# Block 0 of a hybrid layer on one core: who computes the convolution taps, when the transposes run, who scales the norms, and the order of the first norm

## The reference

```
h  = rmsnorm(x, g_mix_pre)
z  = h @ w_in                                   # GLU value | gate | q | k | v | o | i | f
a  = z[GLU value] * sigmoid(z[GLU gate])
a  = causal depthwise conv, width 31 (a) + b    # 512 channels
a  = silu(group_layernorm(a, 4 groups of 128 channels))
hm = group_layernorm(mLSTM(q, k, v, i, f), per head) * sigmoid(o)   # 4 heads, chunkwise
x += rmsnorm(concat(a, hm) @ w_out)
```

## Time and profile before

| | us |
|---|---|
| median of 3 runs | 2807.46 |
| lowest, highest | 2803.95, 2808.06 |
| the profiled execution, its own time | 2811.34 |
| its span in the profile | 2809.4 |
| PE busy | 2710.0 (96%) |
| DVE busy | 1701.6 (61%) |
| ACT busy | 914.6 (33%) |
| POOL busy | 225.7 (8%), all in block 0 |

### The profile page before, as it was taken

The page is one execution under the profiler, slowest core; times in us unless marked ns, Lnnn a source line. Parts: engine busy times, 40 slices in busy tenths (PEclk is TensorE's granted clock), DMA queues, the critical chain, the costliest instruction groups (busy, mean ns, idle before and its releaser), DMA issues.

```text
span 2809.4 us, 37471 instructions
## 1 busy us (share of the span) xinstructions
PE 2710.0 (96%) x14657; PEld 2605.9 (93%) x14657; DVE 1701.6 (61%) x3648; ACT 914.6 (33%) x1851; POOL 225.7 (8%) x93
## 2 busy tenths in 40 slices
PE   6989999999999999999999999999999999899998
PEld 6879999988999999998999999999999998799998
DVE  6976677775646846536566655555766636472644
ACT  5344433444532112424321223443112325211113
POOL 4322433412000000000000000000000000000000
PEclk9999999999999999999999999999999999899999
DMA  8746889987456666574666666556666576366665
GB/s 283 284 158 244 314 324 337 327 301 265 179 214 232 232 230 234 200 278 163 227 231 231 234 225 220 227 201 225 229 236 224 213 279 143 128 249 227 237 226 194
DMA packets 109563, 660.57 MB, mean 235 GB/s; under 512 B 20283, under 2 KB 20927, under 8 KB 39631
## 3 DMA queue, kind: packets, MB, share of 16 engines
q1 hardware_dynamic: 100238, 628.84, 62.6%
q10 hardware_dynamic: 9152, 29.36, 2.8%
HBM read 533.04 MB, written 125.11 MB: 234 GB/s over the span
## 4 chain that ended last, share of the span: by engine, by line
PE 74%; DVE 8%; DMA 8%; ACT 4%; POOL 3%; issue 1%; POOLq 0%; SPq 0%; DVEq 0%; ACTq 0%
PE proj L635 23%; PE proj L636 22%; PE proj L637 22%; DMA w_raw<-in_w_units 7%; POOL w_split L619 3%; ACT w_split L990 1%; DVE mix_room L1578 1%; DMA w_split<-w_kept 1%; DVE cv L1700 1%; PE m L752 1%; DVE small L1797 1%; PE m L668 1%; PE m L792 1%; DVE w_split L2162 1%; PE m L798 1%
## 5 line engine op out<-in xcount | busy, mean ns | idle before, releaser
L635 PE MATMUL proj<-h_split,w_split 128*128 128x416 f32 x2720 | 977.6, 359 | 22.0 <-DVE h_split L1583 7.1
L636 PE MATMUL proj<-h_split,w_split 128*128 128x416 f32 x2720 | 953.9, 351 | 0.0
L637 PE MATMUL proj<-h_split,w_split 128*128 128x416 f32 x2720 | 948.6, 349 | 0.0
L635 PE MATMUL proj<-f_split,w_split 128*128 128x416 f32 x1568 | 565.1, 360 | 32.9 <-DVE f_split L1832 11.6
L636 PE MATMUL proj<-f_split,w_split 128*128 128x416 f32 x1568 | 552.5, 352 | 0.0
L637 PE MATMUL proj<-f_split,w_split 128*128 128x416 f32 x1568 | 549.2, 350 | 0.0
L635 PEld LDWEIGHTS proj<-h_split,w_split 128*128 128x128 f32 x2720 | 511.2, 188 | 37.6 <-issue 19.9
L637 PEld LDWEIGHTS proj<-h_split,w_split 128*128 128x128 f32 x2720 | 512.1, 188 | 9.8
L636 PEld LDWEIGHTS proj<-h_split,w_split 128*128 128x128 f32 x2720 | 512.7, 188 | 3.0 <-issue 0.8
L635 PEld LDWEIGHTS proj<-f_split,w_split 128*128 128x128 f32 x1568 | 296.2, 189 | 54.1 <-DVE f_split L1832 15.1
L1700 DVE SCALAR_TENSOR_TENSOR cv<-a_ext,vecs,cv 128x416 f32<-128x416 f32 (+1 forms) x510 | 315.2, 669 | 0.0
(11 more groups left out here) (270 smaller groups left out, 2184.8 us busy)
## 6 DMA issues: line engine op xcount, KB each, us to landing
w_split<-w_kept SPq DMA_DIRECT2D x432, 1024.0 KB, 4.8
w_kept<-w_split SPq DMA_DIRECT2D x108, 1024.0 KB, 7.8
w_raw<-in_w_units SPq DMA_DIRECT2D x108, 512.0 KB, 5.7
x_resid<-in_x ACTq DMA_DIRECT2D x5, 1664.0 KB, 12.5
out_y<-x_resid ACTq DMA_DIRECT2D x8, 832.0 KB, 9.0
rows<-in_x ACTq DMA_DIRECT2D x4, 832.0 KB, 8.1
w_raw<-in_x ACTq DMA_DIRECT2D x3, 832.0 KB, 11.5
qkv<-in_p ACTq DMA_DIRECT2D x5, 416.0 KB, 5.3
```

The lines of the kernel that those rows point to most:

```text
L635: mm(dst, w_hi, a_hi, start=first, stop=False)
L636: mm(dst, w_hi, a_lo, start=False, stop=False)
L637: return mm(dst, w_lo, a_hi, start=False, stop=last)
```

## The change

It has four parts, all in block 0.

1. *Convolution.* The first 15 taps of channel tile 3 go from PE to DVE; PE keeps 16, now 3, 4, 3, 3 and 3 in the five places instead of 6, 8, 5, 6 and 6. DVE adds PE's sum to its own. Until tap 21, 20 and 10 the partial sums of tiles 0, 1 and 2 lie in the PSUM banks m1, m3 and m4, which the heads need from step A of head 0 on; PE waits for that there (`s_taps`).
2. *Transposes.* T1 moves from group 20 to group 21, behind step A of head 2; within group 23, T2 moves later by two products. Its first transpose waits for all four convolution tiles.
3. *Norm scaling.* ACT scales half of batch 0 and all three tiles of batch 1 (`shifted`), which needs a shift computed by DVE.
4. *First norm.* DVE makes the low part of weight unit 0 in place of POOL; ACT makes the high part of unit 1 ahead of the high parts of h; scaling and low parts alternate; groups 0 and 1 are computed product by product in turn; a small square root at the start of ACT's list loads its table.

```diff
-TURNS_FIRST, TURNS, TURNS_LAST = {"T1": 20, "T2": 23}, {"T1": 17, "T2": 20}, {"T1": 17, "T2": 21}
+TURNS_FIRST, TURNS, TURNS_LAST = {"T1": 21, "T2": 23}, {"T1": 17, "T2": 20}, {"T1": 17, "T2": 21}
+PRODUCTS_FROM = 15
-PRODUCTS_CONV = (range(6), range(6, 14), range(14, 19), range(19, 25), range(25, CW))
+PRODUCTS_CONV = (range(15, 18), range(18, 22), range(22, 25), range(25, 28), range(28, CW))
+TAPS_BANK = [(c, k) for n in range(5) for c, k in ((0, 16 + n), (2, 2 * n), (1, 16 + n), (2, 2 * n + 1))] + [(0, 21), (2, 10)]
+BANK_END = {0: 21, 1: 20, 2: 10}
-TURN_ENDS = (22, 28, 36, 43, 49, 57, 61)
+TURN_ENDS = (8, 14, 24, 31, 37, 47, 54)
...
+            two_groups(0, False, 0, h, lambda n: pe.wait_ge(s_h.sem, s_h.done(0, n + 1)))
             for i in range(FRONT):
-                group(0, False, i, h, ...)
+                if i > 1:
+                    group(0, False, i, h)
...
                     pe.wait_ge(s_evac.sem, s_evac.done(blk, 12 + 3 * i + 3))
+                    if first and i == 0:
+                        pe.wait_ge(s_taps.sem, len(BANK_END))
...
+                    if split and i == 2:
+                        shifted(0, (2, 3))
+                    elif split and i == H - 1:
+                        shifted(1, (5, 6))
...
+                def tap_first(c, k, last_of):
+                    bank = {0: m1, 1: m3, 2: m4}.get(c)
+                    end = BANK_END.get(c, -1)
+                    home, kept = (bank[:, 0:T] if k < n else cv[:, c, :] for n in (end, end + 1))
...
+                        ins = v.scalar_tensor_tensor(home, a_ext[:, c, k:k + T], wt, kept, ALU.mult, ALU.add)
...
+                    if part == len(TURN_ENDS) - 1:
+                        dve.wait_ge(s_convp.sem, 1)
+                        v.tensor_tensor(cv[:, DIAGONAL, :], cv[:, DIAGONAL, :], m5[:, 0:T], ALU.add).then_inc(s_conv.sem, 1)
...
                     inverse_root(0)
+                    dve.wait_ge(s_hi.sem, 1)
+                    v.tensor_tensor(w[:, 0, 1, :], w_raw[:, 0, :], w[:, 0, 0, :].bitcast(F32),
+                                    ALU.subtract).then_inc(s_w[0].sem, 16)
                     dve.wait_ge(s_rb.sem, s_rb.done(blk, 1))
-                    normalise_next(0, range(KD))
+                    for i in range(KD + 4):
+                        if i < KD:
+                            v.scalar_tensor_tensor(x_next(i), x_next(i), col("g_mix_pre", i), m2[:, 0:T], ...)
+                        if i >= 4:
+                            low_next(0, [i - 4])
...
                     batch_stats(0)
+                    batch_factor(0)
+                    batch_apply(0, (0, 1))
                     head_c(2)
```

More of the change, by code:

```diff
@@ L620, in low_part @@
                                         ALU.subtract).then_inc(s_w[slot].sem, 16)
-            for r in range(SPLITS):
+            for r in range(1, SPLITS):
                 if r not in SPLIT_ON_VECTOR:
@@ L870, in program @@
                             for c in range(CT):
-                                then[min(2 * c + 2, KD - 1) if last else 2 * c] = lambda c=c: turn(c)
+                                late = last or first and i == turns["T2"]
+                                then[min(2 * c + 2, KD - 1) if late else 2 * c] = lambda c=c: turn(c)
                         if last and i in (17, 20, 23):
@@ L1060, in _ @@
             root(0, 0, m5, 1)
+            high_part(1)
             for i in range(KD):
                 high_h(0, 0, 0, i, h, x_next(i))
-            for u in range(1, RING):
+            for u in range(2, RING):
                 high_part(u)
@@ L1070, in _ @@
                 front_group(0, 0, i, True)
[L1071 removed]
+                diagonals(range(PRODUCTS_FROM + 2 * i, min(PRODUCTS_FROM + 2 * i + 2, CW)))
             gate_rows(0, 0)
@@ L1115, in shifted @@
                 def shifted(batch, tiles):
-                    act.wait_ge(s_lnshift.sem, batch + 1)
+                    act.wait_ge(s_lnshift.sem, (2 if last else 0) + batch + 1)
+                    if split and batch == 0:
+                        act.wait_ge(s_ln.sem, s_ln.done(blk, 2))
                     for k, (tile, n, size) in enumerate(pieces_of(batch, last)):
@@ L1122, in shifted @@
                         ins = fn(src, src, ACT.Identity, bias=ln_shift[0:size, k:k + 1], scale=ln_rs[0:size, k:k + 1])
-                        if n == (4 if batch else NCH - 1):
+                        if n == (4 if batch and last else NCH - 1):
                             ins.then_inc(s_ln.sem, 1)
@@ L1249, in program @@
                             next_squares(range(6, KD))
-                        elif last and i == 1:
+                        elif not mid and i == 1:
                             shifted(1, (4,))
@@ L1811, in batch_factor @@
                     link(v.reciprocal(ln_rs[0:LC, 0:n], ln_std[0:LC, 0:n]))
-                    if last and batch < 2:
+                    if not mid and batch < 2:
                         v.scalar_tensor_tensor(ln_shift[0:LC, 0:n], ln_mv[0:LC, 0:n, 0], -1.0, ln_rs[0:LC, 0:n], ALU.mult,
@@ new lines, in program @@
+                    head_b(2)
+                    batch_stats(0)
+                    batch_factor(0)
+                    batch_apply(0, (0, 1))
+                    head_c(2)
+                    for c in range(2):
+                        low_mix(c)
+                    batch_stats(1, 0, 2 * NCH)
+                    for c in range(2, CT):
+                        low_mix(c)
+                    head_a(3)
+                    batch_stats(1, 2 * NCH)
+                    head_b(3)
+                    batch_factor(1)
```

190 lines of the change are left out of this document (94 added, 96 removed), and 2 rows, old and new, of the table MIX_FIRST.

## The result

The changed kernel takes 2794.78 us, the median of 5 runs (2792.26 to 2796.61), against 2807.46 before; the ratio is 0.9946, 95% interval 0.9931 to 0.9961. Repeated twice on chips 2 and 5, it gave 2795.09 (ratio 0.9954, 0.9942 to 0.9966) and 2795.65 (0.9949, 0.9930 to 0.9968). The profiled execution took 2796.61, its span is 2794.1. I go through the stages in the order of the forecast.

The account below looks back on a forecast made before the run. PE, busy 96% of the span, was taken as the bound, with VectorE bounding the changed mix. First silu -7.4, batch 1 and head 3 -1.0, clock +1.7: -6.7 from 2807.46 gives 2800.8; 8-in-10 range 2795.5 to 2806.

Parts of the forecast that it names:

- First norm, -3.5: Opening of block 0: PE's first product near 20.1 us instead of 23.58, a gain of 3.5.
- Front, -2.3: 24 to 100 us: both PE waits go, less 0.5 for group 14's evacuation, 2.3 more; step A products near 96.1.
- PSUM taps: VectorE's 22 front taps with sums in PSUM: 0.57 us each, not held up by POOL.
- Convolution complete at 153.5: Mix, on VectorE: 58.3 us of taps, head steps and POOL hold-ups from 95.3, complete at about 153.5.
- seven POOL operations of 2.1 (14.7): Mix: each of seven POOL operations costs VectorE 2.1 us, 14.7 of its 58.3.
- Wait of 5.2 ahead of T1 and the clock's fall behind it, +1.7: Group 21: PE waits 5.2 us at the first transpose; half of a 3.4 us clock fall costs 1.7.
- Scaling gives back 5.1: Before first silu: step B of head 2 comes 12.5 earlier, but silu at 175.0 instead of 182.36, only 7.4 earlier.
- the sharing of batch 1 and head 3: ScalarE scaling batch 1, and step B of head 3 no longer waiting for batch 1's statistics: -1.0.
- Later stages keep their lengths: From silu on the later stages keep their lengths, as no buffer holds more than three units ahead.
- rival A: VectorE held up less, 1.2 per POOL operation: convolution 6 us earlier, -10 to -12, 2796.5; chance 20%.
- C: Time at which the convolution is complete, forecast 153.5; silu starts 21.5 behind it.
- rival B: Half the gain: weights hold up the opening, clock falls again in group 23, VectorE 1 late; -3.5, 2804.0; chance 27%.

Follow-up runs that it names:

- a relief of 5.3: The changed kernel with POOL's seven subtractions of 102 to 151 us (weight units 17 to 23) on 8 of 1024 columns: 2795.1 us.

## Why the prediction was off

The direction was right; the size was half. Of the 6.0 that are missing from the forecast (12.7 against 6.7), the mean of three profiles each puts 3.6 ahead of the sum of the second norm (10.3 against 6.7) and 2.4 behind it, where I had nothing and where the runs can't tell a gain from chance.

- *First norm, -3.5.* Right as a stretch: -3.8. In time the part is worth more, 6.1 alone and 5.2 in the changed kernel; the rest is within the spread of the executions.
- *Front, -2.3.* Step A's products start at 96.14, forecast 96.1; but 2.3 counted two waits of one execution of the kernel before. Its three profiles have these products at 102.2, 101.4 and 101.0, the changed one's at 96.1, 96.4 and 95.9: 5.4 on the mean, so 1.6 in the front. That ScalarE's fewer diagonals are the cause is not shown. Part of this hit was luck.
- *PSUM taps.* Right: 0.65 at most, and the Trainium skill's fixed cost ("VectorE: DVE Perf Modes", TRN2 errata) is again not to be seen: 0.644 at the median with the sum in PSUM, 0.643 for the three taps that read it there and write SBUF, 0.641 in SBUF. (In each of them the other input lies in SBUF.)
- *Convolution complete at 153.5.* This failed. It was 148.0 (150.2 and 148.5 in the other profiles). The term that was wrong is "seven POOL operations of 2.1 (14.7)": measured from 93.1 to 148.0, the operation at 93.11 cost 2.2 and the six behind it 5.3, together 7.5 or 1.07 each. In exchange VectorE waits 4.5 for ScalarE, which I had at nothing, so 2.7 of the 5.5 come from here. Another 2.2 come from the front, by the same mistake: I had taken over the 13.5 of the gate rows with three collisions in them, and there were two. (The second profile had three again, and is complete 2.2 later.) The price of one full collision was right; the mistake was to multiply it by the number of operations. POOL starts when ScalarE has finished the high part, mostly when a group has ended, and then VectorE is often in a head's step that reads PSUM, or waits.
- *Wait of 5.2 ahead of T1 and the clock's fall behind it, +1.7.* Both absent, since PE came to the transposes at 149.2 (forecast 148.3) and found the convolution complete. Step B of head 2 gained 16.9 instead of 12.5.
- *Scaling gives back 5.1.* It gave back 5.8 (from -16.9 to -11.1), by the mechanism named. But I had in this sum, without drawing the conclusion, that ScalarE's 8 pieces and then silu's table come behind VectorE's 8: sharing batch 0, the part that was to help, costs 7 to 8 up to the sum of the second norm (210.4 against 203.3 and 202.1). For the sharing of batch 1 and head 3 I had -1.0; with batch 1 back on VectorE the sum of the second norm is at 210.4 as against 210.2 to 212.3, so the runs do not show it.
- *Later stages keep their lengths.* Right within what can be told.

So it was rival A that came: I had written it with 1.2 per POOL operation, C 6 earlier, PE's wait shrunk to nothing and 2796.5. That its time is near is partly luck, for it has no fall of the clock. The clock did fall, 6.8 us at half in group 23, at the end of PE's wait for silu (4.68): that was a condition of rival B, which had PE waiting some 4 us there.

The trace of before held the answer. I had priced every operation by the seven taps that took 6.12. VectorE's other groups of taps, 20, 8 and 8 of them, and POOL beside the last two and in the head's steps between:

```profile
93.35 17.70 DVE L1717 SCALAR_TENSOR_TENSOR cv<-a_ext,vecs,cv 128x416 f32<-128x416 f32 x20
...
118.28 5.03 DVE L1717 SCALAR_TENSOR_TENSOR cv<-a_ext,vecs,cv 128x416 f32<-128x416 f32 x8
...
145.18 6.03 DVE L1717 SCALAR_TENSOR_TENSOR cv<-a_ext,vecs,cv 128x416 f32<-128x416 f32 x8
```

```profile
116.11 2.81 POOL L619 TENSOR_TENSOR w_split<-w_raw,w_split 128x1024 fp32r<-128x1024 f32 x1 [8.88 <-ACT w_split L990]
127.67 2.41 POOL L619 TENSOR_TENSOR w_split<-w_raw,w_split 128x1024 fp32r<-128x1024 f32 x1 [8.74 <-ACT w_split L990]
...
144.47 2.35 POOL L619 TENSOR_TENSOR w_split<-w_raw,w_split 128x1024 fp32r<-128x1024 f32 x1 [8.08 <-ACT w_split L990]
154.09 2.36 POOL L619 TENSOR_TENSOR w_split<-w_raw,w_split 128x1024 fp32r<-128x1024 f32 x1 [7.27 <-ACT w_split L990]
```

Twenty taps without a pause are 6.2 over their plain 11.5 and have three operations beside them, so 2.1 each. In the mix eight taps are 4.6: the operation at 116.11 costs 0.4, that at 133.98 2.1, that at 144.47 1.4, and those at 127.67 and 154.09 next to nothing, since VectorE was waiting. That is 3.9 for five, 0.8 each. The six taps at their plain 3.46 are no evidence in either direction: no operation ran beside them.

## What to carry to other kernels

A hold-up that two engines cause each other is priced by how often they meet, not by how often one of them runs: count, in the trace, the groups that paid and those that did not. Before an engine is called the bound, ask what it waits for once its load is taken away; 3.7 us of a relief of 5.3 went into waits here. And work shared between two engines gains only if both halves can start together: look at the semaphore and at the table load between them.

## What the runs showed of the hardware

- The three-operand tap on VectorE with its sum in PSUM is not held up by POOL's subtraction at all (48 of 48 at 0.651 or less); with the sum in SBUF it takes up to 2.87. In this kernel this alone is worth 9 us (2804.16 against 2794.8 to 2795.7).
- It is not always VectorE that waits: at 107.30 POOL's operation took 4.34 instead of 2.4 while six SBUF taps ran beside it in their plain 3.46.
- Executions of one kernel differ by 5 to 15 us wherever it ran six times or more (the kernel before: 2801.98 to 2815.67 in 20 runs), and its profiles differ in where the clock is at half. The three profiles of the kernel before differ by 9.5 behind the change, so a difference of one pair of profiles there is no evidence below some 10 us.
